# A hybrid decoder trunk on one core: head sums and broadcasts packed in quarters of TensorE, the rotation's swap by DMA, three of layer 1's gates without their meta columns

## The reference

```python
# retention: q and k are rotated; each head is 64 wide, half = 32
x1, x2 = xh[..., :half], xh[..., half:]
return jnp.concatenate([x1 * cos - x2 * sin, x1 * sin + x2 * cos], axis=-1).reshape(b, l, w)
# mLSTM: one denominator for each head and query
den = jnp.sum(s, axis=-1) + w_inter * jnp.einsum('bhnqd,bhnd->bhnq', qc, n_prev)
h_cell = num / jnp.maximum(jnp.abs(den), jnp.exp(-m_t))[..., None]
# GLA, mLSTM and retention: mean square over each head's 64 channels, then a gate
yh = yh * lax.rsqrt(jnp.mean(yh * yh, axis=-1, keepdims=True) + NORM_EPS)
y_gla = _head_rmsnorm(o, norm_g, GLA_HEADS) * jax.nn.silu(r)
y_ml  = jax.nn.sigmoid(o_pre) * _head_rmsnorm(_from_chunks(h_cell), norm_g, ML_HEADS)
y_ret = jax.nn.silu(g) * _head_rmsnorm(y, norm_g, RET_HEADS)
```

## Time and profile before

| | |
|---|---|
| median of 3 runs | 1015.05 (1014.41 to 1016.66) |
| the profiled execution's own time | 1014.39 |
| its span in the profile | 1012.6 |
| busy time of PE (TensorE) | 982.7 (97% of the span), 7664 matmul instructions |
| DVE, ACT, POOL busy | 592.2, 520.7, 128.1 |
| the chain that ended last | PE 92%, DVE 4%, ACT 2%, issue 1%, DMA 1% |
| granted TensorE clock, mean | 0.991 |
| moved by DMA | 156.42 MB, mean 154 GB/s |

### The profile page before, as it was taken

The page is one execution under the profiler, slowest core; times in us unless marked ns, Lnnn a source line. Parts: engine busy times, 40 slices in busy tenths (PEclk is TensorE's granted clock), DMA queues, the critical chain, the costliest instruction groups (busy, mean ns, idle before and its releaser), DMA issues.

```text
span 1012.6 us, 19561 instructions
## 1 busy us (share of the span) xinstructions
PE 982.7 (97%) x7664; PEld 931.5 (92%) x7664; DVE 592.2 (58%) x870; ACT 520.7 (51%) x826; POOL 128.1 (13%) x106
## 2 busy tenths in 40 slices
PE   7999999999998999999989999999999899999997
PEld 5999888789997999999969998888999899999996
DVE  6556565346966655553465565744579656666443
ACT  4553754366466544454455437544754755454452
POOL 1000000002540222110000000000034212222010
PEclk9999999999999999999989999999999999999998
DMA  5874434246552655555545544344465536555551
GB/s 157 271 229 130 128 120 126 84 125 160 174 169 82 206 167 166 170 191 162 163 125 164 169 139 125 112 126 126 125 162 172 167 125 187 186 183 190 188 187 42
DMA packets 168523, 156.42 MB, mean 154 GB/s; under 512 B 9091, under 2 KB 167022, under 8 KB 168078
## 3 DMA queue, kind: packets, MB, share of 16 engines
q1 hardware_dynamic: 167598, 152.13, 48.7%
q10 hardware_dynamic: 672, 3.37, 1.0%
q0 software_dynamic: 192, 0.07, 0.0%
HBM read 154.50 MB, written 1.05 MB: 154 GB/s over the span
## 4 chain that ended last, share of the span: by engine, by line
PE 92%; DVE 4%; ACT 2%; issue 1%; DMA 1%; SPq 0%; DVEq 0%; ACTq 0%
PE banks L622 26%; PE banks L624 25%; PE banks L623 25%; PE banks L672 2%; PE banks L657 1%; PE banks L653 1%; PE banks L654 1%; PE banks L868 1%; DVE lo L1377 1%; PE banks L870 1%; ACT hi L1039 1%; PE banks L897 1%; PE banks L905 1%; DVE term L1648 1%; DMA xt<-in_x 1%
## 5 line engine op out<-in xcount | busy, mean ns | idle before, releaser
L622 PE MATMUL banks<-xh,hi 128*128 128x272 f32 (+1 forms) x1584 | 460.1, 290 | 2.4 <-DVE lo L1377 1.3
L1377 DVE TENSOR_TENSOR lo<-raw,hi 128x1024 fp32r<-128x1024 f32 (+1 forms) x290 | 356.4, 1232 | 174.8 <-ACT hi L1039 173.6
L624 PE MATMUL banks<-xh,lo 128*128 128x272 f32 (+1 forms) x1584 | 452.9, 286 | 0.0
L623 PE MATMUL banks<-xl,hi 128*128 128x272 f32 (+1 forms) x1584 | 452.8, 286 | 0.0
L1039 ACT ACTIVATE hi<-raw 128x1024 fp32r<-128x1024 f32 (+1 forms) x290 | 302.0, 1042 | 96.5 <-PE banks L624 58.0
L622 PEld LDWEIGHTS banks<-xh,hi 128*128 128x128 f32 x1584 | 298.5, 188 | 9.5 <-issue 6.6
L623 PEld LDWEIGHTS banks<-xl,hi 128*128 128x128 f32 x1584 | 298.0, 188 | 0.6
L624 PEld LDWEIGHTS banks<-xh,lo 128*128 128x128 f32 x1584 | 298.5, 188 | 0.0
L624 PE MATMUL banks<-ah,lo 128*128 128x272 f32 (+1 forms) x352 | 100.4, 285 | 0.0
L622 PE MATMUL banks<-ah,hi 128*128 128x272 f32 (+1 forms) x352 | 100.1, 284 | 0.0
L623 PE MATMUL banks<-al,hi 128*128 128x272 f32 (+1 forms) x352 | 99.9, 284 | 0.0
(11 more groups left out here) (252 smaller groups left out, 1176.4 us busy)
## 6 DMA issues: line engine op xcount, KB each, us to landing
raw<-in_w_in SPq DMA_DIRECT2D x54, 1024.0 KB, 5.2
raw<-in_ffn_w_gate SPq DMA_DIRECT2D x22, 1024.0 KB, 5.3
raw<-in_ffn_w_up SPq DMA_DIRECT2D x22, 1024.0 KB, 5.3
raw<-in_ffn_w_down SPq DMA_DIRECT2D x16, 1024.0 KB, 5.1
raw<-in_w_out SPq DMA_DIRECT2D x8, 1024.0 KB, 5.2
raw<-in_w_in SPq DMA_DIRECT2D x12, 512.0 KB, 4.4
raw<-in_w_branch SPq DMA_DIRECT2D x12, 512.0 KB, 5.6
raw<-in_ffn_w_down SPq DMA_DIRECT2D x8, 768.0 KB, 4.3
```

Of the source, the lines that this page charges most:

```text
L622: mm(dst, wh, mh, start=start, stop=False)
L623: mm(dst, wh, ml, start=False, stop=False)
L624: return mm(dst, wl, mh, start=False, stop=stop)
L1377: tt(lo[g % 2][:, 0:k, f], raw[g % 2][:, 0:k, f], hi[g % 2][:, 0:k, f].bitcast(F32), ALU.subtract).then_inc(lo_ready, 2 if g in G_MIX else 1)
```

## The change

1. **Rotation.** The four matmuls with `perm` are gone. Behind the loads of the groups rv and sbq, SP issues four DMAs for `rq` and four for `rk`, each of 32 partitions x 2 x 272, from the one 32-row block to the other, into `sa` and `sb2`. DVE's `rot` waits for these four and multiplies in SBUF. `sb_scores` waits for `rot_done`.
2. **Denominators.** Each head has a quarter of TensorE's columns and of the bank's rows (row 32h). Four matmuls of 272 columns, four of 256 and four of 128 take the place of nine, and wait for all heads' `pt` first. `ml_em` leaves its result in rows 32 to 35, and ACT issues four DMAs of one row each that put them in rows 0, 32, 64 and 96, which `den_abs` waits for; DVE first fills that part of `rows` with ones.
3. **Mean squares.** Eight matmuls with 32 output rows each, in two rounds of four quarters, take the place of six with 12.
4. **Broadcasts.** One step behind logit 19 issues all six, two that read 64 rows and four that read 32, into six banks.
5. **Layer 1.** gr, rg and mo are computed for the 256 real columns, and what follows them in `y_rest`, `round_y` and `rest_of_y` too.

```diff
+QUERY_ONLY = ("gr", "rg", "mo")
+SWAP_BEHIND = {"rv": "rq", "sbq": "rk"}
+def head_row(pair, i):
+    return 32 * (2 * pair + i) if pair < 2 else 32 * (pair - 2) + 1 + i
...
-    19: [("headbc", 0)],
-    20: [("headbc", 1)],
...
-    24: [("headbc", 5)],
+    19: [("headbc",)],
...
+        spread_banks = [banks[:, 2 + p, :] for p in range(6)]
+        def group_start(l, name):
+            return q_start(l) if name in QUERY_ONLY else 0
...
+            def swap(l, name):
+                for j in range(2):
+                    wait_taken(sp, group_tile(l, name) + j)
+                for at in range(0, P, HD):
+                    for to, src in ((at, at + 32), (at + 32, at)):
+                        sp.dma_start(turned_of(name)[to:to + 32, :, 0:T], M[name][src:src + 32, :, :]).then_inc(swapped[name], 16)
...
             def group(l, name):
...
-                    features(t + j, g, j, xh, xl, 0)
+                    features(t + j, g, j, xh, xl, group_start(l, name))
...
-            def rot(l, i):
...
-                mm(rot_banks[i % 2][:, 0:T], cut["perm"], M[name][:, i % 2, :], start=True, stop=True).then_inc(rot_ready[l], 1)
...
             def sb_scores(l, i):
-                pe.wait_ge(rot_free[l], 4)
+                pe.wait_ge(rot_done[l], 4)
...
             def ml_den(l):
-                den = c3("denind", 4)
-                wait_p(l, ML, 0)
-                mm(e0[0:4, 0:T], cut["denind0"], M["pt0"][:], start=True, stop=False)
                 for h in range(HEADS):
                     wait_p(l, ML, h)
-                    mm(e0[0:4, KB1:T], den[:, h, :], M["pt"][:, h, 0:256], start=False, stop=False)
-                    last = mm(e0[0:4, KB2:T], den[:, h, :], M["pt"][:, h, 256:SCW], start=False, stop=h == 3)
+                for h in range(HEADS):
+                    mm(e0[quad[h], 0:T], cut["denind"][quad[h], :], M["pt0"][quad[h], :], start=True, stop=False)
+                for h in range(HEADS):
+                    mm(e0[quad[h], KB1:T], cut["denind"], M["pt"][:, h, 0:256], start=False, stop=False)
+                for h in range(HEADS):
+                    last = mm(e0[quad[h], KB2:T], cut["denind"], M["pt"][:, h, 256:SCW], start=False, stop=True)
...
             def headsum(l):
+                for g in range(HEADS):
+                    mm(ps[quad[g], 0:T], total[:, g % 2, :], osq[:, g // 2, :], start=True, stop=False)
+                for g in range(HEADS):
+                    last = mm(ps[quad[g], 0:T], total[:, 2, :], osq[:, 2 + g, :], start=False, stop=True)
...
+            def headbc(l):
+                for p in range(6):
+                    rows = slice(HD * p, HD * p + HD) if p < 2 else quad[p - 2]
+                    mm(spread_banks[p][:, 0:T], c3("headbc", 6)[rows, p, :], M["rows"][rows, 0, :], start=True, stop=True).then_inc(spread_ready[l], 1)
...
             def ml_em_(l):
-                act.wait_ge(ml_dve[l], 11)
-                fn(M["rows"][0:4, 1, :], M["rows"][32:36, 0, :], ACT.Exp, scale=-1.0).then_inc(ml_em, 1)
+                act.wait_ge(ml_dve[l], 12)
+                fn(rows[32:36, 0, :], rows[32:36, 0, :], ACT.Exp, scale=-1.0).then_inc(ml_em, 1)
+                act.wait_ge(ml_em, l + 1)
+                for h in range(HEADS):
+                    act.dma_start(rows[32 * h:32 * h + 1, 1, :], rows[32 + h:33 + h, 0, :]).then_inc(em_spread, 16)
...
             def rot(l, i):
-                dve.wait_ge(rot_ready[l], i + 1)
-                tt(turned, rot_banks[i % 2][:, 0:T], cut["sin"], ALU.mult).then_inc(rot_free[l], 1)
+                dve.wait_ge(swapped[name], 64 * (l + 1))
+                tt(turned, turned, cut["sin"], ALU.mult).then_inc(rot_sin[l], 1)
...
             def ml_rows(l):
+                dve.wait_ge(ml_dve[l], 10)
+                nc.vector.memset(rows[:, 1, :], 1.0).then_inc(ml_dve[l], 1)
```

More of the change, by code:

```diff
@@ L120, in constants @@
     c["sin"][:] = np.tile(np.concatenate([-np.sin(ang), np.sin(ang)]), (2, 1))
-    other = np.where(p % HD < half, p + half, p - half)
-    c["perm"][other, p] = 1
+    c["headsum"][:HD, 0] = c["headsum"][HD:, 32] = 1.0 / HD
+    c["headsum"][:HD, 64 + 1] = c["headsum"][HD:, 64 + 2] = 1.0 / HD
     for pair in range(6):
         for i in range(P):
-            j = 2 * pair + i // HD
-            c["headsum"][i, pair * 12 + j] = 1.0 / HD
-            c["headbc"][j, pair * P + i] = 1
+            c["headbc"][head_row(pair, i // HD), pair * P + i] = 1
+    c["denind"][:, 0] = 1
     for h in range(HEADS):
-        c["denind"][:, h * 4 + h] = 1
-        c["denind0"][:, h] = head == h
         c["negind"][32 + h, h] = -1
@@ L558, in _ @@
                         load(g, cols(w_in[l], c))
+                    if name in SWAP_BEHIND:
+                        swap(l, SWAP_BEHIND[name])
                     g += 1
@@ L926, in _ @@
             parts = {
-                "first": first, "group": group, "turn": turn, "gate": gate, "rot": rot, "logit": logit, "headsum": headsum, "headbc": headbc,
+                "first": first, "group": group, "turn": turn, "gate": gate, "logit": logit, "headsum": headsum, "headbc": headbc,
                 "sb_scores0": sb_scores0, "sb_scores": sb_scores,
@@ L1108, in group @@
                     elif name in ("gr", "rg"):
-                        ins = fn(M[name][:, j, :], ps, ACT.Silu)
+                        ins = fn(M[name][:, j, q0:], ps, ACT.Silu)
                     elif name == "sbq":
-                        ins = fn(M["sbq"][:, j, :], ps, ACT.Copy, scale=HD ** -0.5)
+                        ins = fn(M["sbq"][:, j, q0:], ps, ACT.Copy, scale=HD ** -0.5)
                     elif name in V_OF:
@@ L1114, in group @@
                     else:
-                        ins = fn(M[name][:, j, :], ps, ACT.Copy)
+                        ins = fn(M[name][:, j, q0:], ps, ACT.Copy)
                     taken(ins, t + j)
@@ L1219, in den_abs_ @@
                 act.wait_ge(den_ready, l + 1)
-                act.wait_ge(ml_em, l + 1)
-                fn(M["rows"][0:4, 0, :], e0[0:4, 0:T], ACT.Abs).then_inc(den_abs, 1)
+                act.wait_ge(em_spread, 64 * (l + 1))
+                fn(M["rows"][:, 0, :], e0[:, 0:T], ACT.Abs).then_inc(den_abs, 1)
             def head_square(l, p):
@@ L1228, in head_rstd @@
             def head_rstd(l):
-                r = M["rows"][0:12, 0, :]
+                r = M["rows"][:, 0, :]
                 wait_taken(act, TILE[l][("headsum",)])
```

72 lines of the change are left out of this document (33 added, 39 removed).

## The result

The changed kernel took 998.88 us (median of 4 runs, 998.42 to 1002.75) beside 1015.86 for the kernel before (4 runs, 1014.41 to 1018.17): a ratio of 0.9839, 95% interval 0.9808 to 0.9871. The profiled execution took 998.42 with a span of 996.5, so 16.1 us less span than before. The forecast was 1000.0, range 998.3 to 1004.2.

A forecast was written before the change was run, and what follows sets the result against it. TensorE, busy 97% of the span, was taken to bound the kernel. Terms 3.67 + 3.60 + 3.60 + 2.74 + 1.38 = 15.0 off the profiled 1014.39 gave 999.4, forecast as a median of 1000.0 us, range 998.3 to 1004.2.

The forecast's parts named there:

- What bounds the kernel: TensorE, busy 97% of the span, without waits where the change touches; time taken from it there comes off the end.
- Rotation: Eight perm matmuls, two pairs a layer, leave TensorE at 0.459 each: 3.67 us saved, the transfers replacing them costing nothing.
- Denominators: Three rounds of four quarters in the denominators take 1.35 us instead of 3.15: 1.80 saved a layer, 3.60 in all.
- Mean squares: Two rounds of four quarters take 1.05 us instead of 2.85: 1.80 saved a layer, 3.60 in all.
- Broadcasts: Two packed rounds at 0.59 each plus shape changes, 1.38 us against 2.75: 1.37 saved a layer, 2.74 in all.
- Layer 1's columns: In gr, rg and mo of layer 1, 144 matmuls get 0.0096 us shorter each: 1.38 saved.
- What is added elsewhere: ACT's four DMA issues behind ml_em, 0.35 us each, leave it 0.2 to 0.65 late; hidden until logit 8, costing nothing.
- The swap: The swap of rq behind rv's load lands at 73.4 us, before DVE reaches the rotation at 74.57; no wait.
- the slower rival: Late swaps hold up DVE at the rotation; landing by 80.0 costs TensorE nothing; total over 1017 us, chance 0.02.
- Four quarters are four times as wide: Forecast's claim for packed rounds; its rival, four run as two and two, gives up to 1004.1 us, chance 0.18.
- one bank and one row tile at a time: Rival: the denominators' first round, into one bank, runs one by one, saving 2.8 us less: 1002.8, chance 0.04.
- DVE's pace behind the broadcasts: Rival: DVE needs 3.04 us a step against TensorE's 2.79 in layer 1; 1.6 lost, 1001.6, chance 0.08.

The follow-up runs named there:

- experiments 7: Changed kernel with the six broadcasts not packed (all 128 rows each) but still in one step, six banks: median 1005.32 us, ratio 0.9906 to the kernel before.
- experiment 8: Changed kernel with the broadcasts alone undone: six single steps, two banks in turn; median 1004.77 us, ratio 0.9894 to the kernel before.
- Experiment 9: Changed kernel with two changes of shape fewer per layer: first denominator round takes 128 rows, denominators right ahead of values; median 996.87 us, ratio 0.9844.
- experiment 10: Changed kernel with the exponent's four rows spread by one DMA instead of four; median 1001.64 us, ratio 0.9867 to the kernel before.
- Experiment 6: Changed kernel with ACT's four one-row exponent DMAs issued twice, the second four into an unread spare tensor; median 1007.23 us, ratio 0.9921.
- experiment 4: Changed kernel with both swaps one load later in the queue (rq behind sbq, rk behind sbk); median 1008.03 us, ratio 0.9919.
- e0: Not a run: the PSUM bank that the denominators' first round writes, four row tiles each into its own quarter of the rows; it has no measured time.
- experiments 5: The changed kernel itself run once more, nothing altered; median 999.38 us, ratio 0.9849 to the kernel before.

## Why the prediction was right, and where it was off

*What bounds the kernel.* Right: what came out of TensorE's stretches came off the span, since no stretch between them grew in return, and undoing an edit put the same us back into them (3.66, 9.30, 1.13; with 14.05 for all at once). The medians rose by more, 5.2, 11.5 and 3.3; in the profiled executions the difference lies in the start and behind the norms.

*Rotation*, 3.67: measured 3.66. *Denominators*, 3.60: 3.55. *Mean squares*, 3.60: 3.59 (the content is 1.80 less in layer 0, 1.79 in layer 1).

*Broadcasts*, 2.74: mis-sized. The matmul behind the packed step starts 211.87 - 210.54 = 1.33 after it, entering costs 210.54 - 210.32 - 0.126 = 0.09, leaving 0.10, in all 1.52 and not 1.38. The term "0.59 each" came from `ret_scores0` with 32 columns of weights; a round with 128 columns takes 0.66, half of 1.33. I had counted one change of shape a round, but all four passes take 0.33, also the second of each round, whose shape is the same as the first's; such a second pass takes 0.23 in the mean squares, with 32 columns of weights. What holds up each pass with 128 columns by 0.10 isn't shown. Against 2.75 the step saves 1.22 a layer (experiments 7 and 8: 1.22 twice, 1.20 and 1.31), 2.44. Experiment 9 prices the changes of shape themselves: the denominators' first cost 0.13 (1.38 - 1.25) and the return to the stream ahead of `values` the other 0.19 of 0.32.

*Layer 1's columns*, 1.38: 1.13, because p in layer 1 is 0.118 and not 0.1163. The step was that one row stood for the pitch of all of layer 1. The same 0.3 us of that stage, left open in experiment 8, makes layer 1's stretch behind `headsum` 2.71 shorter, where the mean squares and experiment 8 give 1.79 + 1.31.

*The sum*: 15.0 forecast, 14.05 found (the terms one by one add to 14.37, and the open 0.3 is between the two); but 16.1 by the spans. The difference of 1.9 hid the miss of 0.95, and that was luck: start and norms fell well for the execution profiled, with 1.11 in the start and 1.27 behind layer 1, where the clock fell in the profiled execution of the kernel before and not in that of the changed one. Without that the forecast of 1000.0 should have come out near 1001; in three sittings the changed kernel and its twin of experiment 10 had 998.9, 999.4 and 1001.6.

*What is added elsewhere.* The cost of nothing was right; two of its working figures were not. An issue on ACT takes 0.76 and not 0.35, so ACT is 2.3 late and not 0.2 to 0.65, and the step "the bank is wanted by logit 8" overlooked `take_out` 2, which stands on ACT's list between logits 6 and 7 and frees the bank for `values(1,1)`. The margin left was 0.5. Experiment 6 shows what lay behind it.

*The swap.* That DVE doesn't wait was right, but by luck. I had the swap start when the load of rv lands, 70.7, and take 2.7: there at 73.4, 1.2 ahead of DVE. In fact SP issues it from 64.91 on, and it takes 4.6 to 4.9. In experiment 4 all four were there 7.22 after the first began to be issued (71.21 to 78.43); here that gives 72.1 as an estimate, 1.2 ahead of DVE's 73.37 again. Two errors cancelled; from 70.7 on, 4.6 would have made DVE wait. The bound worked out under the slower rival, 80.0, was not contradicted where experiment 4 comes near it: the swap of `rq` landed at 78.43, with TensorE's stream 0.9 earlier and the first rotation pair gone from it, and cost TensorE nothing. The 2.32 came with that of `rk`, for which the prediction worked out no bound of its own.

*The rivals.* Four quarters are four times as wide, with four streams of 128 rows too. For one bank and one row tile at a time see L859: four row tiles write bank `e0`, each its own quarter of the rows, and eight instructions last 0.66 together. The rule of the Trainium skill, "TensorEngine Tiling (Array Packing)", Restrictions and Gotchas, that different row tiles cannot access the same PSUM bank at the same time, is not what this chip did; the measurement decides. For a gain of less than four the answer depends on the columns of the weights. With 32, the denominators' round of four row tiles costs 0.59 with a change of shape, and 0.46 without the 0.13 of that, so all of the gain is there. With 128, the broadcasts' round of four row tiles costs 0.67 (211.20 to 211.87), and 4 x 0.459 / 0.67 is 2.7. The Trainium skill, "TensorE: Matmul & The Clock Gate", Part 3, gives 3.07 for four row tiles. The denominators' round doesn't show such a loss and the broadcasts' shows a somewhat larger one; the prediction had set the figure aside by rows with 32 columns only. For DVE's pace behind the broadcasts: no wait for it appears.

## What to carry to other kernels

When one engine is full, price an edit by the pitch of its instructions in the stretch itself, and check it by the same stretch afterwards; two executions of one program differ here by more than a small edit is worth. A packed round of 32 weight columns costs its moving columns once, and beside that its change of shape, 0.13 here; with 128 weight columns every pass cost 0.10 more. Put rounds of one shape together, and next to work that changes shape anyway, and take the price from a row with as many weight columns. For work that another engine takes on, list everything behind it on that engine and look for the first thing that the full engine needs, not for the one that comes to mind: the margin here was 0.5 us, and a stall can cost more than its length.

## What the runs showed of the hardware that I had not expected

Small transfers inside SBUF are dear to issue and slow to land: 0.61 to 0.85 of the issuing queue's time each (2.69 for four on SP, 2.44 to 3.39 for four on ACT), against 0.35 for a load of constants in the earlier trace rows, and 4.6 to 4.9 for 68 KB, where 1 MB from HBM needs 5.2. One DMA of four rows costs 0.63, as much as one of one row.

In experiment 6 a stall of 2.37 in TensorE's stream is followed by about 10 us at a mean granted clock of 0.58 and 0.74, and so costs 5.6; that of 2.01 in layer 1 costs 6.8. The stall of 2.3 in experiment 4 isn't followed by that: there the clock stays at 1.00 in the windows of 5 us around and behind it, and the stretch loses 2.96 in all. It need not be the kernel that tells the two apart. The wait of 2.8 for the norm behind layer 1, the same in all thirteen profiled executions, was followed by the lower clock in nine and not in four, and the kernels of experiments 5 and 10, which have the same instructions there, are one of either kind. What decides it in one execution stays open.
